# Order of the mixer stage in a two-layer hybrid decoder step: second maxima, first sample's sum, local value loads and gmlp squares moved

## The chip, the cores and the metric

The kernel runs on one core of a Trainium2 chip. The metric is the device time of one execution in microseconds (us). Engines are named TensorE (PE), VectorE (DVE), ScalarE (ACT), GpSimd (POOL) and SyncE (SP), as in the rows; PEld is TensorE's weight load and SPq is SyncE's queue, which issues transfers. All is float32; the large products are split into a high and a low part.

## The reference, cut to what matters

One step of a decoder trunk with two layers. A prompt of 256 tokens and 8 samples with one new token each go through it together. Every layer is FFN, mixer, FFN. The mixer has one input projection and four head groups of 256 channels: A dilated window attention, B attention with forget gates (FoX), C a gated delta rule, D a gated MLP over positions (gmlp). A sample attends to 1024 cached positions.

```python
h = rms_norm(x, g[2]);  parts = project(h, w_in)
# A, sample: keys at distances 0, d, 2d.. < window for (128,1), (512,4), (2048,16), merged by their denominators
o_a = combine_by_denominator([dilated_sample(qa, ka_all, va_all, wb, w, d) for (w, d) in DILATED_PATTERNS])
# B, sample: 8 pages of 128 cached rows, found by page_table, and the own row
o_b = fox_attend(qb, kb_all, vb_all, cum_t, cum_t[:, :, past:], pos)
# C: short convolution, L2 norms, chunked delta rule with a triangular inverse; returns the new state
o_c, s_c, conv_c = gdn_branch(qc, kc, vc, ac, bc, gdn_conv, gdn_s, conv_w, a_log, dt_b)
# D: u = gelu(ud); v = rms_norm(gelu(vd), gv); u * (W_s v + b)
o_d, v_d = gmlp_branch(ud, vd, ws, bs, gv)
y = merge_groups(o_a, o_b, o_c, zc, o_d, out_g, w_out)      # norm per head, gate, output product
```

Outputs are the new activations, and keys, values, gates and states of the prompt and the samples.

## The kernel before

Five engines run one program each, written out by hand in `build`; nothing schedules them but the order of the code and waits on counting semaphores. `S(name)` is a semaphore and `V(name, n)` its value n in this layer. `ch(...)` waits until the instruction in it is done.

FFN stages: weights come in pieces of 1 MB on SyncE's queue, ScalarE makes their high part (L610), VectorE the low part (L1026), and TensorE does three products (L1586 to L1588).

The mixer stage follows the input projection. Its prompt part is on TensorE and VectorE: scores of B and of A in banks 0 to 3 of PSUM, `row_max(0)` and `row_max(1)` on VectorE (L1275 to L1283), `softmax` on ScalarE, transposes of the probabilities on TensorE (L1830) with copies back (`probs_out`, L1289), `delta_front` (L1378 to L1386), `attend_scale` (L1297), and then six levels of the triangular inverse (`LEVELS`). In each level TensorE does y products (L1946), VectorE masks them (L1467), TensorE does z products (L1957, L1958), VectorE subtracts (L1475, L1476). The tables `masked` and `between` name what VectorE does behind the masks and behind the subtractions of each level; `after_y` and `after_z` do so for TensorE.

The sample part is threaded through it. Keys and values of a sample are 11 tiles of 128 rows: 8 pages of the FoX cache, and 3 window tiles of the local cache (`window`, L452 to L454). There are two buffers for keys (`kslot`) and two for values (`vslot`), by sample parity. The work on samples:
- SyncE: `read_pages(b)` reads 8 page numbers into registers (L433); `keys(b)` waits until `s_red` says that the sums of sample b-2 are done, then sends the queries (L474), 8 pages (L462) and 3 window tiles; `vals(b)` waits until `pv_mm` says that TensorE is done with the buffer, then sends 8 pages (L470) and 3 window tiles.
- GpSimd multiplies keys and queries (L1001 to L1004), sample by sample.
- VectorE sums over each head: `sample_add(b)` (L1325, L1327). Then, for pairs j of samples, `sample_bias(j)`, `sample_top(j)`, `sample_shift(j)`.
- ScalarE: `sample_exp(j)` (L785).
- TensorE: `sample_values(j)` (L1898, L1900), after the exponentials and after `v_in0` and `v_in1` say that all 11 value tiles of both samples have landed. It is in `after_z` of levels 1, 3 and 5 for j = 0, 1, 2, and behind the levels for j = 3.
- VectorE: `sample_out(j)` (L1365 to L1367).

For the samples' own key and value VectorE does ten small instructions (L1307 to L1316), between `row_max(0)` and `row_max(1)`. They write `v_own` and `sx`. The gmlp branch needs the sum of squares of v: `gmlp_square` (L1411 to L1415) on VectorE, root on ScalarE (L808, L809), then `gmlp_norm` (L1421 to L1429) on VectorE, its last four instructions for the samples. ScalarE does the squares of the head outputs (L821 to L833) between `sample_exp(1)` and `sample_exp(2)`. The convolution of the samples is scaled by VectorE (L1405) and stored by SyncE (L521), and comes back in other layouts with the states (L525 to L530). SyncE stores keys and values of the prompt (L514 to L517) ahead of `keys(2)`.

Of the kernel before, what the change touches and what calls it, by code (L numbers as in the profile page):

```python
# [23 lines left out]
P = 128  # L24
# [4 lines left out]
B = 8  # L29
# [35 lines left out]
def constants():  # L65
# [71 lines left out]
    "lf_turned": 1, "logf_in": 16, "logf_pre": 1024, "max_diag": 4, "max_turned": 4, "mix_d": 2, "mix_r": 7, "mix_ready": 8, "mix_ss": 6, "mixed": 3, "mm_done0": 77,  # L137
# [13 lines left out]
def build(nc, io):  # L151
# [14 lines left out]
    with ctx:  # L166
# [181 lines left out]
        with nc.Block() as blk:  # L348
            @blk.sync
            def _(sp):  # L350
# [9 lines left out]
                for l in range(DEPTH):  # L360
# [152 lines left out]
                    sp.wait_ge(S("rope"), V("rope", 2))  # L513
                    sp.dma_start(pr(o["fox_k_prompt"][0, l]), tok[:, :, KB_:KB_ + GW]).then_inc(st, 16)  # L514
                    sp.dma_start(pr(o["fox_v_prompt"][0, l]), tok[:, :, VB_:VB_ + GW]).then_inc(st, 16)
                    sp.dma_start(pr(o["swa_v_prompt"][0, l]), tok[:, :, VA:VA + GW]).then_inc(st, 16)
                    sp.dma_start(pr(o["swa_k_prompt"][0, l]), tok[:, :, KA:KA + GW]).then_inc(st, 16)  # L517
# [23 lines left out]
                    vals(5)  # L541
                    sp.dma_start(sm(o["fox_k_sample"][:, l]), smp[:, KB_:KB_ + GW]).then_inc(st, 16)
# [53 lines left out]
            def _(act):  # L596
                ch = Chain(act, "act_ch")
                for l in range(DEPTH):
# [219 lines left out]
                    act.wait_ge(S("mix_d"), V("mix_d", 2))  # L818
# [16 lines left out]
                    sample_exp(2)  # L835
                    sample_exp(3)

                    act.wait_ge(S("mix_ss"), V("mix_ss", 4))
# [4 lines left out]
                    act.wait_ge(S("mix_ss"), V("mix_ss", 5))  # L843
                    ch(act.activation(small[0:B, 104:108], small[0:B, 104:108], ACT.Ln, bias=C("eps", B), scale=1.0 / HD))
                    act.activation(small[0:B, 104:108], small[0:B, 104:108], ACT.Exp, scale=-0.5).then_inc(S("mix_r"), 1)
                    act.wait_ge(S("mix_ss"), V("mix_ss", 6))
# [41 lines left out]
            def _(pool):  # L888
# [5 lines left out]
                for l in range(DEPTH):  # L894
# [72 lines left out]

                    def skp_of(k):
# [23 lines left out]
                    for b in range(B):  # L992
# [3 lines left out]
                        if b == 4:  # L996
                            skp_of(0)
# [18 lines left out]
            def _(dve):  # L1016
                ch = Chain(dve, "dve_ch")
                for l in range(DEPTH):
# [285 lines left out]
                    dve.wait_ge(S("rope"), V("rope", 2))  # L1304
                    own = v_own[:, 0, 0:GW]
                    for k, (qc, kc) in enumerate(((QB_, KB_), (QA, KA))):
                        ch(tt2(own, smp[:, qc:qc + GW], smp[:, kc:kc + GW], ALU.mult))  # L1307
                        ch(red(small[0:B, 112 + 4 * k:116 + 4 * k], own.rearrange("p (h d) -> p h d", h=H), AX.X, ALU.add))
                    ch(ts(small[0:B, 112:120], small[0:B, 112:120], HD ** -0.5, None, ALU.mult))

                    ch(dve.tensor_copy(sx[:, :, :, :], C("own_bias").rearrange("p (b k h) -> p b k h", b=B, k=2)))
                    ch(tt2(sx[0:B, :, :, :].rearrange("p b k h -> p b (k h)"), sx[0:B, :, :, :].rearrange("p b k h -> p b (k h)"),
                           small[0:B, 112:120].unsqueeze(1).broadcast_to([B, B, 8]), ALU.add))
                    dve.memset(v_own[:, :, GW:GW + 1], 1.0)
                    ch(dve.tensor_copy(v_own[:, 0, 0:GW], smp[:, VB_:VB_ + GW]))
                    dve.tensor_copy(v_own[:, 1, 0:GW], smp[:, VA:VA + GW]).then_inc(S("v_own"), 1)  # L1316
# [77 lines left out]
                    probs_out(1)  # L1394
                    attend_scale(1, 0)
                    sample_add(0)
# [10 lines left out]
                    def gmlp_square():  # L1407

                        dve.wait_ge(S("gelu"), V("gelu", 2))
                        for t in range(NT):  # L1410
                            ch(tt2(kb2[:, 0:GW], tok[:, t, VD:VD + GW], tok[:, t, VD:VD + GW], ALU.mult))  # L1411
# [659 lines left out]
```

## Time and profile before

| what | us |
|---|---|
| median of 3 runs | 1471.14 |
| lowest, highest | 1467.81, 1475.22 |
| the profiled execution | 1459.36 |
| its span in the profile | 1457.5 |
| first mixer stage, in the profile | about 308 to 496 |
| second mixer stage | about 1022 to 1206 |

By engine, busy share of the span: TensorE 88%, VectorE 62%, ScalarE 43%, GpSimd 17%. The profiler's page also has the granted clock of TensorE, mean 0.93 of full speed; it is lower in the mixer stages, where TensorE often stands idle. A timeline row gives the start, the busy time, the engine, the line of the kernel, what is written and read, and in brackets the idle time before it with what ended it. A row that merges several instructions (x8) gives their busy time in sum. In a row of waits the three numbers are us in total, times, and the longest.

### The profile page before, as it was taken

The page shows a single profiled execution, that of the slowest core. Times are in us where ns is not written, and L with a number is a line of the kernel's source. Part 1 is how long each engine was busy: PE and PEld are TensorE (multiplying, and loading weights), DVE is VectorE, ACT ScalarE, POOL GpSimd, SP SyncE. Part 2 cuts the span into 40 slices and gives each one's busy share as a digit, 9 for nine tenths or more (in the row PEclk, how much of TensorE's full clock was granted, in tenths as well). Part 3 has the DMA queues.
Part 4 walks back from the last instruction along what each step waited for, and adds up shares of the span by engine and source line. Part 5 has one row for each costly group of instructions (what it writes and reads, how often), then busy time and mean ns, then how long its engine had stood idle before and what let it go on. Part 6 is the DMA issues. An engine that isn't in the chain of part 4 may idle for free.

```text
span 1457.5 us, 27836 instructions
## 1 busy us (share of the span) xinstructions
PE 1282.8 (88%) x9956; PEld 1196.2 (82%) x9956; DVE 903.6 (62%) x1512; ACT 619.8 (43%) x1151; POOL 242.0 (17%) x250
## 2 busy tenths in 40 slices
PE   6999999995755899999999999999676579999998
PEld 5999998984633499999989999999565338899996
DVE  3776447868844557664477663586877454776644
ACT  4655355453020265443465553543612004644443
POOL 2000011025456030000110000110635531100000
PEclk9999999998877699999999999999978767999998
DMA  7555565534456435554655555655435643455563
GB/s 233 163 184 174 147 173 172 174 110 105 143 178 191 141 103 186 178 187 139 187 176 178 173 173 160 188 159 172 115 110 175 186 151 125 138 173 184 154 172 96
DMA packets 286121, 234.17 MB, mean 161 GB/s; under 512 B 19898, under 2 KB 282018, under 8 KB 286056
## 3 DMA queue, kind: packets, MB, share of 16 engines
q1 hardware_dynamic: 286056, 233.37, 52.7%
q8 instruction: 33, 0.54, 0.2%
q14 instruction: 32, 0.26, 0.1%
HBM read 228.65 MB, written 5.37 MB: 161 GB/s over the span
## 4 chain that ended last, share of the span: by engine, by line
PE 71%; DVE 15%; SPq 5%; issue 4%; ACT 3%; DMA 2%; DVEq 0%; ACTq 0%
PE ps L1586 20%; PE ps L1587 20%; PE ps L1588 19%; DVE wlo L1026 2%; PE ps L1898 2%; SPq L470 2%; SPq L462 1%; DVE nlo L1080 1%; DVE s L1325 1%; DVE ps L1063 1%; ACT whi L610 1%; PE ps L1957 1%; DMA vslot<-in_state_swa_v_dram 1%; DMA raw<-in_w_in_dram 1%; PE ps L1923 1%
## 5 line engine op out<-in xcount | busy, mean ns | idle before, releaser
L1586 PE MATMUL ps<-nhi,whi 128*128 128x264 f32 x1936 | 559.5, 289 | 19.3 <-DVE wlo L1026 11.4
L1587 PE MATMUL ps<-nlo,whi 128*128 128x264 f32 x1936 | 552.1, 285 | 0.0
L1588 PE MATMUL ps<-nhi,wlo 128*128 128x264 f32 x1936 | 551.5, 285 | 0.0
L1026 DVE TENSOR_TENSOR wlo<-raw,whi 128x1024 fp32r<-128x1024 f32 (+2 forms) x364 | 380.7, 1087 | 268.3 <-ACT whi L610 267.8
L610 ACT ACTIVATE whi<-raw 128x1024 fp32r<-128x1024 f32 (+2 forms) x364 | 324.9, 942 | 165.7 <-PE ps L1588 104.7
L1586 PEld LDWEIGHTS ps<-nhi,whi 128*128 128x128 f32 x1936 | 368.1, 190 | 28.9 <-DVE nlo L1080 14.4
L1587 PEld LDWEIGHTS ps<-nlo,whi 128*128 128x128 f32 x1936 | 368.5, 190 | 0.2
L1588 PEld LDWEIGHTS ps<-nhi,wlo 128*128 128x128 f32 x1936 | 366.6, 189 | 0.0
L1586 PE MATMUL ps<-hhi,whi 128*128 128x264 f32 x704 | 203.1, 288 | 9.1 <-DVE hlo L1048 9.1
L1588 PE MATMUL ps<-hhi,wlo 128*128 128x264 f32 x704 | 202.2, 287 | 0.0
L1587 PE MATMUL ps<-hlo,whi 128*128 128x264 f32 x704 | 201.8, 287 | 0.0
L1586 PEld LDWEIGHTS ps<-hhi,whi 128*128 128x128 f32 x704 | 134.6, 191 | 10.0 <-issue 9.8
L1588 PEld LDWEIGHTS ps<-hhi,wlo 128*128 128x128 f32 x704 | 134.9, 192 | 0.0
L1587 PEld LDWEIGHTS ps<-hlo,whi 128*128 128x128 f32 x704 | 134.7, 191 | 0.0
L901 POOL TENSOR_TENSOR ss_acc<-sq 128x264 f32<-128x264 f32 x12 | 9.1, 757 | 726.7 <-ACT sq L640 674.6
L630 ACT ACTIVATE hhi<-h_t 128x264 f32 (+1 forms) x88 | 37.4, 425 | 164.2 <-DVE h_t L1045 164.2
L1001 POOL TENSOR_TENSOR kslot<-kslot,q_bc 128x512 f32<-128x512 f32 x64 | 82.1, 1313 | 113.1 <-DMA kslot<-in_state_swa_k_dram 113.1
L905 POOL TENSOR_TENSOR ss_acc<-ss_acc,sq 128x264 f32<-128x264 f32 x66 | 56.7, 860 | 187.7 <-ACT sq L640 166.0
L1898 PE MATMUL ps<-vslot,s 128*4 128x257 f32 x352 | 41.2, 487 | 44.9 <-DMA vslot<-in_state_swa_v_dram 44.9
L1048 DVE TENSOR_TENSOR hlo<-h_t,hhi 128x264 f32 (+1 forms) x88 | 38.2, 434 | 59.9 <-ACT hhi L630 59.9
L1898 PEld LDWEIGHTS ps<-vslot,s 128*4 128x4 f32 x352 | 12.9, 98 | 68.4 <-issue 60.6
L785 ACT ACTIVATE s<-s 128x104 f32<-128x104 f32 x8 | 2.3, 290 | 156.8 <-DVE s L1358 156.8
(345 smaller groups left out, 1465.6 us busy)
## 6 DMA issues: line engine op xcount, KB each, us to landing
raw<-in_ffn_gate_dram SPq DMA_DIRECT2D x44, 1024.0 KB, 5.3
raw<-in_ffn_up_dram SPq DMA_DIRECT2D x44, 1024.0 KB, 5.4
raw<-in_ffn_down_dram SPq DMA_DIRECT2D x64, 704.0 KB, 4.5
raw<-in_w_in_dram SPq DMA_DIRECT2D x24, 1024.0 KB, 5.7
kslot<-in_cache_fox_k_dram SPq DMA_DIRECT2D x128, 128.0 KB, 2.8
vslot<-in_cache_fox_v_dram SPq DMA_DIRECT2D x128, 128.0 KB, 2.8
raw<-in_w_out_dram SPq DMA_DIRECT2D x8, 1024.0 KB, 5.1
kslot<-in_state_swa_k_dram SPq DMA_DIRECT2D x32, 128.0 KB, 2.8
```

Source lines behind the costliest of these rows:

```text
L462: sp.dma_start(kslot[:, i, g, :], io["cache_fox_k"][bass.ds(page_of[b, g], 1), l].rearrange("o p h d -> p (o h d)")).then_inc(S(f"k_in{i}" ...
L470: sp.dma_start(vslot[:, i, g, 0:GW], io["cache_fox_v"][bass.ds(page_of[b, g], 1), l].rearrange("o p h d -> p (o h d)")).then_inc(S(f"v_in{ ...
L610: act.activation(whi[s][:, a:b], raw[s][:, a:b], ACT.Copy).then_inc(S(f"w_hi{s}"), 1)
L630: act.activation(hhi[:, bass.ds(2 * j + f, 1), :].rearrange("p o n -> p (o n)"), h_t[:, f, :], ACT.Copy).then_inc(S("h_hi"), 1)
L905: ins = tt_(ss_acc[:, :], ss_acc[:, :], sq8[:, t, :], ALU.add)
L1001: ins = tt_(kslot[:, i, g:g + 2, :], kslot[:, i, g:g + 2, :], q_bc[:, i, GW:512].unsqueeze(1).broadcast_to([P, 2, GW]), ALU.mult)
L1026: tt2(wlo[s][:, a:b], raw[s][:, a:b], whi[s][:, a:b].bitcast(F32), ALU.subtract).then_inc(S(f"w_lo{s}"), 1)
L1048: tt2(hlo[:, at, :].rearrange("p o n -> p (o n)"), h_t[:, f, :], hhi[:, at, :].rearrange("p o n -> p (o n)").bitcast(F32), ALU.subtract).t ...
L1586: mm(out, wh, hi_, start=first, stop=False)
L1587: mm(out, wh, lo_, start=False, stop=False)
L1588: return mm(out, wl, hi_, start=False, stop=last)
L1898: mm(out, s13[:, u, FOX_PG * m + g, :], vslot[:, i, NPG * m + g, :], start=(g == 0), stop=False)
```

## The change

Nothing is computed in another way, but for the samples' squares of the gmlp branch, which are summed in two halves. In every layer:
- VectorE does `row_max(1)` directly behind `row_max(0)` and the bias copies. The ten instructions for `v_own` stand behind `probs_out(1)` instead, ahead of `attend_scale(1, 0)`.
- `sample_add(0)` stands ahead of `probs_out(0)` instead of behind `attend_scale(1, 0)`. In the tables, `sample_add(2)` and `(3)` move to level 1, `(4)` to level 2, `(5)` to level 3 and `(6)` to level 4.
- The window tiles of the values for samples 2 to 7 are issued by ScalarE, behind `sample_exp(0)`, `(1)` and `(2)`, each time after a wait for `pv_mm`. SyncE issues them for samples 0 and 1 alone.
- SyncE does `read_pages(6)` and `keys(3)` ahead of the convolution's store, `keys(4)` behind it, `keys(5)` ahead of `vals(2)` and `keys(6)` behind `vals(3)` and ahead of `read_pages(7)`. The prompt's keys and values are stored behind `vals(5)`.
- ScalarE does the gmlp squares with an accumulating output, right behind the root for the convolution, and scales the samples' v. GpSimd does the rest of the samples' gmlp ahead of its product for sample 3 (`b == 3`). The state product `skp_of(0)` moves from `b == 4` to `b == 6`.

```diff
@@ SyncE @@
-                        window(vslot, i, b, "state_swa_v", S(f"v_in{i}"))
+                        if not use:
+                            window(vslot, i, b, "state_swa_v", S(f"v_in{i}"))
...
-                    sp.wait_ge(S("rope"), V("rope", 2))
-                    sp.dma_start(pr(o["fox_k_prompt"][0, l]), tok[:, :, KB_:KB_ + GW]).then_inc(st, 16)
...
                     read_pages(5)
                     keys(2)
+                    read_pages(6)
+                    keys(3)
                     sp.wait_ge(S("s_conv"), V("s_conv", 1))
                     sp.dma_start(d_cn.rearrange("c b (h e) -> (c b h) e", h=H), cv[:, 8, :]).then_inc(S("regroup"), 16)
-                    keys(3)
+                    keys(4)
...
-                    read_pages(6)
-                    keys(4)
+                    keys(5)
                     vals(2)
-                    keys(5)
                     vals(3)
+                    keys(6)
                     read_pages(7)
-                    keys(6)
                     keys(7)
                     vals(4)
                     vals(5)
+                    sp.wait_ge(S("rope"), V("rope", 2))
+                    sp.dma_start(pr(o["fox_k_prompt"][0, l]), tok[:, :, KB_:KB_ + GW]).then_inc(st, 16)
...
@@ ScalarE @@
-                    act.wait_ge(S("mix_ss"), V("mix_ss", 3))
-                    ch(act.activation(small[:, 24:27], small[:, 24:27], ACT.Ln, bias=C("eps"), scale=1.0 / GW))
-                    act.activation(small[:, 24:27], small[:, 24:27], ACT.Exp, scale=-0.5).then_inc(S("mix_r"), 1)
+                    for t in range(NT):
+                        act.activation(kb_n[:, t, :], tok[:, t, VD:VD + GW], ACT.Square, accum_out=small[:, 24 + t:25 + t])
...
+                    act.activation(smp[:, VD:VD + GW], smp[:, VD:VD + GW], ACT.Copy, scale=small[0:B, 26:27]).then_inc(S("mix_r"), 1)
+
+                    def value_windows(j):
+
+                        act.wait_ge(S("pv_mm"), V("pv_mm", j))
+                        for i in range(2):
+                            a = io["state_swa_v"][2 * j + i, l].rearrange("r h d -> r (h d)")
+                            sem = S(f"v_in{i}")
+                            act.dma_start(vslot[:, i, NPG, 0:GW], a[PAST - P:PAST, :]).then_inc(sem, 16)
...
                     sample_exp(0)
+                    value_windows(1)
                     act.wait_ge(S("state_in"), V("state_in", 16 * (B + 4 + 2 + 4)))
                     act.activation(small[:, 120:121], gb[:, 0:1], ACT.Exp).then_inc(S("sg"), 1)
                     sample_exp(1)
+                    value_windows(2)
...
                     sample_exp(2)
+                    value_windows(3)
                     sample_exp(3)
@@ GpSimd @@
-                        if b == 4:
+                        if b == 3:
+                            sample_gmlp()
+                        if b == 6:
                             skp_of(0)
@@ VectorE @@
+                    sample_add(0)
                     probs_out(0)
                     delta_front()
                     probs_out(1)
+                    dve.wait_ge(S("rope"), V("rope", 2))
+                    own = v_own[:, 0, 0:GW]
...
                     attend_scale(1, 0)
-                    sample_add(0)
...
-                    masked = {0: [lambda: add(1), lambda: sample_bias(0)], 1: [lambda: sample_shift(0)], 2: [lambda: out(0), lambda: add(3), lambda: sample_bias(1)],
-                              3: [lambda: sample_shift(1), lambda: add(4)], 4: [lambda: out(1), lambda: add(5), lambda: sample_bias(2)],
-                              5: [lambda: sample_shift(2), lambda: add(6)]}
-                    between = {0: [lambda: sample_top(0), conv_scale, gmlp_square], 1: [gmlp_norm, lambda: add(2)], 2: [lambda: sample_top(1), gmlp_mix],
-                               3: [lambda: state_sum(0)], 4: [lambda: sample_top(2), state_value], 5: [state_new]}
+                    masked = {0: [lambda: add(1), lambda: sample_bias(0)], 1: [lambda: sample_shift(0), lambda: add(2)], 2: [lambda: out(0), lambda: sample_bias(1)],
+                              3: [lambda: sample_shift(1), lambda: add(5)], 4: [lambda: out(1), lambda: sample_bias(2)], 5: [lambda: sample_shift(2)]}
+                    between = {0: [lambda: sample_top(0), conv_scale], 1: [lambda: add(3), gmlp_norm], 2: [lambda: sample_top(1), lambda: add(4), gmlp_mix],
+                               3: [lambda: state_sum(0)], 4: [lambda: sample_top(2), lambda: add(6), state_value], 5: [state_new]}
```

The built programs show the order on the engines. First VectorE at the head of the mixer, before; `s_115` is the tile `s13` of the samples' sums, `proj` holds the second scores, `ptr` the probabilities:

```order
L1303 COPY bias<-const 128x8x12
L1307 TENSOR_TENSOR v_own<-smp 8x256
...
L1316 COPY v_own<-smp 8x256
L1281 SCALAR_TENSOR_TENSOR proj<-ps,const 128x1536
L1282 TENSOR_REDUCE small<-proj 128x4
L1283 TENSOR_REDUCE small<-proj 128x4
L1391 COPY proj<-ps 128x4x128
L1289 COPY ptr<-ps 128x512 x3
L1378 TENSOR_TENSOR tt<-ps,ys 128x2x2x64 x2
```

and the same place with the change:

```order
L1338 COPY bias<-const 128x8x12
L1316 SCALAR_TENSOR_TENSOR proj<-ps,const 128x1536
L1317 TENSOR_REDUCE small<-proj 128x4
L1318 TENSOR_REDUCE small<-proj 128x4
L1413 COPY proj<-ps 128x4x128
L1347 TENSOR_REDUCE s_115<-kslot 128x32
L1349 TENSOR_REDUCE s_115<-kslot 128x12
L1324 COPY ptr<-ps 128x512 x3
L1400 TENSOR_TENSOR tt<-ps,ys 128x2x2x64 x2
...
L1324 COPY ptr<-ps 128x512
L1421 TENSOR_TENSOR v_own<-smp 8x256
```

The maxima (three rows on `proj`) follow the bias copy, the two sums of `sample_add(0)` stand ahead of the three probability copies, and `v_own` comes behind the fourth.

ScalarE behind the root for the convolution, before:

```order
L805 ACTIVATE small<-small 64x1
L808 ACTIVATE small<-small,const 128x3
L809 ACTIVATE small<-small 128x3
L785 ACTIVATE s_115<-s_115 128x104
L813 ACTIVATE small<-gb 128x1
L785 ACTIVATE s_115<-s_115 128x104
L821 ACTIVATE ptr,small<-otok 128x64 x24
```

and with the change:

```order
L817 ACTIVATE smp<-smp,small 8x256
L786 ACTIVATE s_115<-s_115 128x104
L825 DMA vslot<-in_state_swa_v_dram 128x256
L826 DMA vslot<-in_state_swa_v_dram 128x256
L827 DMA vslot<-in_state_swa_v_dram 64x256
...
L832 ACTIVATE small<-gb 128x1
L786 ACTIVATE s_115<-s_115 128x104
...
L842 ACTIVATE ptr,small<-otok 128x64 x24
```

Six transfers now stand behind each of the first three exponentials (those on `s_115`), ahead of the exponential of the gate and of the squares of the heads.

## Rows read from the trace of the kernel before

**Rows 1.** Who waited for whom, 320 to 500 us, first mixer stage.

```profile
POOL kslot L1001 <- DMA kslot<-in_state_swa_k_dram: 58.2, 6, 24.0
...
PE ps L1898 <- DMA vslot<-in_state_swa_v_dram: 23.6, 2, 13.0
```

**Rows 2.** The waits of SyncE's queue, 330 to 500 us.

```profile
SPq L474 <- DVE s L1327: 21.5, 3, 14.6
...
SPq L470 <- PE ps L1900: 5.4, 1, 5.4
```

**Rows 3.** Timeline of VectorE, first mixer stage.

```profile
334.14 0.98 DVE L1307 TENSOR_TENSOR v_own<-smp 8x256 f32<-8x256 f32 x1
...
342.65 1.74 DVE L1281 SCALAR_TENSOR_TENSOR proj<-ps,const 128x1536 f32<-128x1536 f32 x1
...
345.02 1.21 DVE L1283 TENSOR_REDUCE small<-proj 128x4 f32<-128x1024 f32 x1
...
360.18 0.69 DVE L1297 TENSOR_TENSOR otok<-ps,small 128x512 f32<-128x512 f32 x1 [2.96 <-PE ps L1845]
...
367.83 0.93 DVE L1327 TENSOR_REDUCE s<-kslot 128x12 f32<-128x768 f32 x1
...
373.47 0.30 DVE L1405 TENSOR_SCALAR cv<-cv,small,const 96x64 f32<-96x64 f32 x1
...
377.28 1.27 DVE L1467 TENSOR_TENSOR ys<-ps,const 128x512 f32<-128x512 f32 x2
```

**Rows 4.** Timeline of GpSimd, end of the product for sample 1.

```profile
346.95 1.26 POOL L1004 TENSOR_TENSOR kslot<-kslot,q_bc 128x512 f32<-128x512 f32 x1
```

**Rows 5.** Timeline of SyncE's queue, first mixer stage: issues, not landings.

```profile
339.12 2.50 SPq L512 DMA_DIRECT2D gb<-d_gate  x4
...
363.95 0.34 SPq L474 DMA_DIRECT2D q_bc<-d_q  x1
...
369.46 0.51 SPq L454 DMA_DIRECT2D kslot<-in_state_swa_k_dram  x1
...
380.60 1.06 SPq L525 DMA_DIRECT2D kq<-d_cn  x2
...
384.15 3.81 SPq L530 DMA_DIRECT2D state<-in_state_gdn_s_dram  x8
...
417.55 0.47 SPq L454 DMA_DIRECT2D vslot<-in_state_swa_v_dram  x1
422.84 0.33 SPq L474 DMA_DIRECT2D q_bc<-d_q  x1
...
429.95 0.50 SPq L454 DMA_DIRECT2D kslot<-in_state_swa_k_dram  x1
...
447.39 3.85 SPq L470 DMA_DIRECT2D vslot<-in_cache_fox_v_dram  x8
...
452.23 0.47 SPq L454 DMA_DIRECT2D vslot<-in_state_swa_v_dram  x1
```

**Rows 6.** Timeline of TensorE: `sample_values(1)` and the start of `sample_values(2)`.

```profile
420.67 3.60 PE L1898 MATMUL ps<-vslot,s 128*4 128x257 f32 x28 [13.01 <-DMA vslot<-in_state_swa_v_dram]
...
428.67 0.70 PE L1900 MATMUL ps<-v_own,s 8*4 8x257 f32 x4
...
455.69 3.59 PE L1898 MATMUL ps<-vslot,s 128*4 128x257 f32 x28 [10.55 <-DMA vslot<-in_state_swa_v_dram]
```

**Rows 7.** Second layer: timelines of SyncE's queue and of TensorE.

```profile
1052.83 2.90 SPq L512 DMA_DIRECT2D gb<-d_gate  x4
...
1166.02 3.59 PE L1898 MATMUL ps<-vslot,s 128*4 128x257 f32 x28 [8.91 <-DMA vslot<-in_state_swa_v_dram]
```

**Rows 8.** Timeline of ScalarE: the squares of the heads and `sample_exp(2)`.

```profile
404.83 0.24 ACT L821 ACTIVATE ptr<-otok 128x64 f32<-128x64 f32 x1
...
412.49 0.41 ACT L833 ACTIVATE small<-small 128x16 f32<-128x16 f32 x3
...
443.83 0.29 ACT L785 ACTIVATE s<-s 128x104 f32<-128x104 f32 x1 [30.93 <-DVE s L1358]
```

More of the change, by code:

```diff
@@ L541, in _ @@
                     vals(5)
+                    sp.wait_ge(S("rope"), V("rope", 2))
+                    sp.dma_start(pr(o["fox_k_prompt"][0, l]), tok[:, :, KB_:KB_ + GW]).then_inc(st, 16)
+                    sp.dma_start(pr(o["fox_v_prompt"][0, l]), tok[:, :, VB_:VB_ + GW]).then_inc(st, 16)
+                    sp.dma_start(pr(o["swa_v_prompt"][0, l]), tok[:, :, VA:VA + GW]).then_inc(st, 16)
+                    sp.dma_start(pr(o["swa_k_prompt"][0, l]), tok[:, :, KA:KA + GW]).then_inc(st, 16)
                     sp.dma_start(sm(o["fox_k_sample"][:, l]), smp[:, KB_:KB_ + GW]).then_inc(st, 16)
@@ new lines, in _ @@
+                    ch(act.activation(st_s[0:B, :, :].rearrange("b a v -> b (a v)"), smp[:, VD:VD + 128], ACT.Square, accum_out=small[0:B, 26:27]))
+                    ch(act.activation(st_s[0:B, :, :].rearrange("b a v -> b (a v)"), smp[:, VD + 128:VD + GW], ACT.Square, accum_out=small[0:B, 27:28]))
+                    ch(act.activation(small[0:B, 26:27], small[0:B, 26:27], ACT.Identity, bias=small[0:B, 27:28]))
+                    act.activation(small[:, 24:26], small[:, 24:26], ACT.Ln, bias=C("eps"), scale=1.0 / GW)
@@ L966, in masks, with sample_gmlp @@
                             C("strict").unsqueeze(1).broadcast_to([P, 8, P]), ALU.mult).then_inc(S("dts"), 1)
+                    def sample_gmlp():
+                        pool.wait_ge(S("mix_r"), V("mix_r", 3))
+                        tt_(smp[:, VD:VD + GW], smp[:, VD:VD + GW], gv[0:B, :], ALU.mult).then_inc(S("gmlp_v"), 1)
+                        pool.wait_ge(S("gmlp_v"), V("gmlp_v", 1))
+                        od = smp_o[:, 768:1024].rearrange("p (h d) -> p h d", h=H)
+                        eight = lambda ap: ap.unsqueeze(2).broadcast_to([B, H, HD])
+                        ch(tt_(od, smp[:, VD:VD + GW].rearrange("p (h d) -> p h d", h=H), eight(ws0[:, 0, :]), ALU.mult))
+                        ch(tt_(od, od, eight(ws0[:, 1, :]), ALU.add))
+                        tt_(smp_o[:, 768:1024], smp_o[:, 768:1024], smp[:, UD:UD + GW], ALU.mult).then_inc(S("mix_s"), 1)
                     def skp_of(k):
@@ L1303, in _ @@
                     dve.tensor_copy(bias[:, :, NPG:NKT, :], C("window").rearrange("p (g h) -> p g h", h=H).unsqueeze(1).broadcast_to([P, B, CACHE_T, H]))
[L1304 to L1316, printed above, removed]
                     row_max(1)
@@ L1394, in _ @@
                     probs_out(1)
+                    dve.wait_ge(S("rope"), V("rope", 2))
+                    own = v_own[:, 0, 0:GW]
+                    for k, (qc, kc) in enumerate(((QB_, KB_), (QA, KA))):
+                        ch(tt2(own, smp[:, qc:qc + GW], smp[:, kc:kc + GW], ALU.mult))
+                        ch(red(small[0:B, 112 + 4 * k:116 + 4 * k], own.rearrange("p (h d) -> p h d", h=H), AX.X, ALU.add))
+                    ch(ts(small[0:B, 112:120], small[0:B, 112:120], HD ** -0.5, None, ALU.mult))
+                    ch(dve.tensor_copy(sx[:, :, :, :], C("own_bias").rearrange("p (b k h) -> p b k h", b=B, k=2)))
+                    ch(tt2(sx[0:B, :, :, :].rearrange("p b k h -> p b (k h)"), sx[0:B, :, :, :].rearrange("p b k h -> p b (k h)"),
+                           small[0:B, 112:120].unsqueeze(1).broadcast_to([B, B, 8]), ALU.add))
+                    dve.memset(v_own[:, :, GW:GW + 1], 1.0)
+                    ch(dve.tensor_copy(v_own[:, 0, 0:GW], smp[:, VB_:VB_ + GW]))
+                    dve.tensor_copy(v_own[:, 1, 0:GW], smp[:, VA:VA + GW]).then_inc(S("v_own"), 1)
                     attend_scale(1, 0)
-                    sample_add(0)
                     dve.wait_ge(S("s_silu"), V("s_silu", 1))
@@ L1405, in conv_scale @@
                         ts(cv[:, 8, :], cv[:, 8, :], small[0:96, 0:1], C("q_scale", 96), ALU.mult, ALU.mult).then_inc(S("s_conv"), 1)
[L1407 to L1411, printed above, removed]
-                            ch(red(small[:, 24 + t:25 + t], kb2[:, 0:GW], AX.X, ALU.add))
-                        ch(dve.memset(small[:, 26:27], 1.0))
-                        ch(tt2(kb2[0:B, 0:GW], smp[:, VD:VD + GW], smp[:, VD:VD + GW], ALU.mult))
-                        red(small[0:B, 26:27], kb2[0:B, 0:GW], AX.X, ALU.add).then_inc(S("mix_ss"), 1)
                     def gmlp_norm():
@@ L1422, in gmlp_norm @@
                         ins.then_inc(S("v_n"), 1)
-                        stt(smp[:, VD:VD + GW], smp[:, VD:VD + GW], small[0:B, 26:27], gv[0:B, :], ALU.mult, ALU.mult).then_inc(S("gmlp_v"), 1)
-                        dve.wait_ge(S("gmlp_v"), V("gmlp_v", 1))
-                        od = smp_o[:, 768:1024].rearrange("p (h d) -> p h d", h=H)
-                        eight = lambda ap: ap.unsqueeze(2).broadcast_to([B, H, HD])
-                        ch(tt2(od, smp[:, VD:VD + GW].rearrange("p (h d) -> p h d", h=H), eight(ws0[:, 0, :]), ALU.mult))
-                        ch(tt2(od, od, eight(ws0[:, 1, :]), ALU.add))
-                        tt2(smp_o[:, 768:1024], smp_o[:, 768:1024], smp[:, UD:UD + GW], ALU.mult).then_inc(S("mix_d"), 1)
                     def gmlp_mix():
@@ L1927, in turned_state @@
                     def turned_state():
-                        pe.wait_ge(S("mix_d"), V("mix_d", 2))
+                        pe.wait_ge(S("mix_d"), V("mix_d", 1))
                         state_mm(0)
```

19 lines of the change are left out of this document (11 added, 8 removed).

## The prediction, made before the run

> **What bounds the kernel now.** I read the views from the outside in. The page's engine rows say TensorE is busy for 88% of the span, but that is a mean over unlike stages: the FFN stages are solid TensorE, and the two mixer stages are not. So I went to the waits of the first layer's mixer, from 320 to 500 us. There the reader is to see two waits for data: GpSimd stands 58.2 us for the sliding-window keys, TensorE 23.6 us for the sliding-window values [rows 1]. Who is late there, the transfers or their issue? The waits of SyncE's queue answer: it stood 21.5 us itself for VectorE's sums over the keys (`sample_add`), the longest time 14.6 us [rows 2]. A key buffer is free only when `sample_add` of two samples earlier is done. VectorE does `sample_add(0)` late, behind work that nothing there needs yet. The mixer is therefore a latency chain: VectorE's order, then key transfers, then products, then sums, then value transfers, then `sample_values`. It ends twice in a transfer: `sample_values(1)` starts at 420.67 and `sample_values(2)` at 455.69, both when a window transfer lands [rows 6].
>
> **The head of the stage, part by part.** VectorE's ten small instructions for the sample's own key and value take from 334.14 to 342.65, 8.5 us, and the second maxima (3.5 us, to 346.15) stand behind them, though their scores are ready [rows 3]. The change puts the maxima first: their end moves from 346.15 to 337.65. Between the maxima and the three probability copies it puts `sample_add(0)`, 3.1 us (before, from the end of L1297 at 360.87 to the free of the buffer at 363.95) [rows 3, 5]. In that gap VectorE waited for TensorE's transposes anyway for some 1.2 us, so the copies end 6.5 us earlier than before rather than 8.5, and the wait for TensorE's next product (1.1 us before) vanishes too: the delta part runs 7.6 us earlier. The ten moved instructions now stand ahead of `attend_scale(1)`, where VectorE idled 2.96 us [rows 3]. What do they cost there? At most 8.5 us as now, at least what fits the idle time, nothing. I take 3.4 us, an estimate from small instructions beside no product, 0.2 to 0.4 us each as L1405's 0.30 [rows 3]: GpSimd's second product ends at 348.2 [rows 4] and the block starts at about 349.5. That leaves 0.5 us uncovered. With `sample_add(0)` gone from behind it, the sum over the head is 7.6 - 0.5 + 3.1 = 10.2 us: `sample_add(1)` ends at 358.5 instead of 368.76 [rows 3].
>
> **The port of the two engines.** One instruction of the head moves into GpSimd's products: L1383, two operands in SBUF, at about 344. The first of the ten, with both operands in SBUF too, took 0.98 us beside GpSimd's work [rows 3]. For L1383 the bounds are nothing and one instruction of GpSimd, 1.26 us [rows 4]; since only this one stands there I count nothing and keep 1.2 us for the range. The Trainium skill (SBUF — State Buffer, Who interferes with whom) says that a VectorE instruction with two SBUF inputs and a GpSimd instruction that reads SBUF exclude each other for a whole instruction. The trace fits it, and by that rule the sum would be 2.4 us smaller over both layers.
>
> **SyncE's queue becomes the bound.** With that head, I lay out SyncE's issues from the end of the gate transfers at 341.62 [rows 5] in their new order. The terms, per layer:
> - page numbers of samples 5, 6, 7: before, the queue stood from 418.02 to 422.84 for one sample's eight, 4.8 us, with its sums long done [rows 5]; 3 x 4.8 = 14.4.
> - six key sets: one is 6.0 us (363.95 to 369.97), the slowest 7.6 (422.84 to 430.45) [rows 5]; the twelve of both layers average 6.3, and I take that: 37.8.
> - four value sets without their window: 3.85 us and a small gap each [rows 5], 15.6. The three window issues of a set, 1.4 us (from 451.24 to 452.70), go to ScalarE.
> - the convolution's store, and the group of keys, values and states (380.60 to 387.96) [rows 5]: 7.8.
> Sum 75.6 us. On top come its waits. Set 3 is ready to issue at 341.62 + 4.8 + 6.3 + 4.8 = 357.5 and waits for `sample_add(1)`: 1.0. Set 4 is ready at 365.2 and waits for `sample_add(2)`, which follows `sample_add(1)` by the 5.0 us to the end of L1405 [rows 3], two masks, the shift and its own 3.1, so at 368.1: 2.9. I round to 4.0. Later sets find their sums done by 4 us or more. Value set 5 is thus issued at 341.62 + 79.6 = 421.2 and lands 3.0 us later, as before (452.70 to 455.69) [rows 5, 6]: `sample_values(2)` starts at 424.2 instead of 455.7, **31.5 us** earlier. In the second layer the queue starts at 1055.73 and the same instruction at 1166.02 [rows 7]; 1055.73 + 82.6 = 1138.3, so **27.7 us**. What follows `sample_values(2)` is unchanged and depends on little else.
>
> **What is moved at no cost, and its cover.** The four prompt outputs (four issues of about 0.5 us) now stand ahead of the last value sets; SyncE waited 5.4 us for TensorE there [rows 2], and pays 2 us if that wait is gone. The squares that VectorE loses (L1411 to L1415, between 373.77 and 377.28) [rows 3] are 3.5 us off VectorE, and the sample's share of the norm goes too, but once SyncE's queue sets the pace, they lie in slack: I count nothing for them. GpSimd takes over four small instructions before its product for sample 3, where it waits for keys; ScalarE does the squares ahead of `sample_exp(0)`, for which it waits anyway. If either cover were gone, the price would be about the 3.5 us that VectorE paid.
>
> **Sum.** 31.5 + 27.7 = 59.2 us off the profiled execution's 1459.4: 1400.2. That execution is 0.8% below the median of the three runs, 1471.1; from the median the same saving gives **1412 us**, which I forecast. A measurement of this kernel can tell about 0.5%, some 7 us, from no change.
>
> **Rivals.**
> - *The transfers, not their issue, set the pace.* With fewer gaps, and ScalarE's windows beside SyncE's sets, every set could take what the slowest took [rows 5]: six times 1.3 and, by the same ratio, four times 0.8, 11 us a layer. The gain is 37.2: 1434. For it: one set did take 7.6; against it: most sets run at the issue's own pace. The Trainium skill (DMA: Bandwidth & Descriptors, Issuing engines are not separate DMA queues) says that all issuing engines share the same 16 DMA engines, and that a second one saves issue time alone. By it the moved windows would be worth their 5.6 us a layer only where the issue bounds. No row of before shows two queues at work.
> - *More than the sum.* The 4 us of waits go, sets take 6.0: 5.8 us a layer more, 1459.4 - 70.8 = 1389 from the faster base.
> - *Only the head is won*, 2 x 10.2, since another wait, say GpSimd for the third product, absorbs the rest: 1451. Against it: the long wait for keys is released by the head itself.
> - *Slower.* ScalarE now waits for TensorE's values and issues six transfers before it may do the head squares and `sample_exp(2)`. The squares take 8.1 us (404.83 to 412.90) [rows 8]. `sample_values(1)`, after value set 3 lands at 399.7, ends by 408.4 even at its 8.7 us of before (420.67 to 429.37) [rows 6]. `sample_exp(2)` is wanted at 424.2, so 15.8 us are there: each issue may cost (15.8 - 8.1)/6 = 1.3 us for nothing. `sample_shift(2)` lets it start no sooner than some 14.3 us after the values anyway (429.4 to 443.83) [rows 8]. SyncE pays 0.47 to 0.51 for such an issue [rows 5], so this is close only if ScalarE is three times as slow. From (7.7 + 29.6)/6 = 6.2 us an issue the gain is gone; at 7 us the kernel is 2 x 4.7 slower: 1481.
>
> **Numbers.** Forecast 0.56 (its own range 1400 to 1424), slower transfers 0.20, more than the sum 0.14, head alone 0.05, ScalarE's queue 0.05, of which 0.03 beyond 0.5% and 0.02 within it. So faster 0.95, same 0.02, slower 0.03. The range is 1388, the stronger case from the faster base, to 1436, slower transfers and the port's 2.4 us; it leaves out the last two cases and a little of each end.
>
> **What would show it.** VectorE's L1281 starts at about 334.1 instead of 342.65. SyncE's first key set starts at about 346.4 instead of 363.95, and the queue runs with gaps of under 3 us to value set 5. `sample_values(2)` starts near 424 and 1138, less in both layers by about 30. GpSimd's long wait of 24.0 us [rows 1] shrinks to some 7. ScalarE's window issues show about 0.45 us each, and none of its waits is followed by a late `sample_exp`. I am wrong if key sets last over 7 us, if TensorE waits for ScalarE before L1898, or if the queue still stands long for sums.

## The result, and the profile after

| us | before | after |
|---|---|---|
| median of all runs | 1469.47 (1462.03 to 1475.22) | **1410.78** (1408.83 to 1412.02) |
| the profiled execution | 1459.36 | 1412.02 |

The ratio is 0.9602, 95% interval 0.9556 to 0.9648: faster, by 58.7 us between the medians. The forecast was 1412 us. But the two profiled executions, against which the sum was made, differ by only 47.3 us, where the sum said 59.2. Both numbers have to be explained.

Busy time by stage, of the kernel before (first mixer, FFN stages between, second mixer, FFN at the end; then the granted clock, DMA share and GB/s):

```profile
308.00:496.00 188.00, 122.47 (x877) 91.51 (x875) 125.51 (x248) 45.46 (x155) 85.28 (x75) 0.79 0.49 142
496.00:1022.00 526.00, 513.56 (x4096) 502.58 (x4095) 324.52 (x504) 260.73 (x412) 35.64 (x46) 0.99 0.55 168
1022.00:1206.00 184.00, 120.37 (x875) 92.12 (x872) 125.96 (x248) 44.66 (x155) 85.03 (x75) 0.80 0.49 145
```

and with the change:

```profile
308.00:469.00 161.00, 120.97 (x881) 91.39 (x880) 111.79 (x237) 48.12 (x167) 86.51 (x81) 0.81 0.60 168
469.00:995.00 526.00, 513.85 (x4095) 502.63 (x4094) 324.49 (x504) 261.15 (x412) 35.71 (x46) 0.99 0.55 168
995.00:1159.00 164.00, 119.56 (x873) 91.57 (x870) 118.09 (x237) 47.88 (x167) 85.35 (x79) 0.83 0.55 162
```

The windows are cut where the products over the heads begin (495.54 and 1205.69 before, 468.67 and 1159.07 after) and 16 us ahead of the second mixer's first queries. The FFN stages are the same 526 us with the same busy times. The first mixer is 27 us shorter, the second 20: only there is something to explain. TensorE's busy share rose from 88 to 91%, with the same work.

Waits, 320 to 500 us, with the change, against [rows 1]:

```profile
POOL kslot L1036 <- DMA kslot<-in_state_swa_k_dram: 35.0, 6, 8.7
PE ps L1915 <- DMA vslot<-in_cache_fox_v_dram: 5.6, 2, 4.4
```

The longest wait for keys fell from 24.0 to 8.7 us, the wait for values from 23.6 to 5.6. SyncE's own waits for the sums, 320 to 500 us, against the 21.5 us of [rows 2]:

```profile
SPq L475 <- DVE s L1349: 5.5, 2, 4.0
```

Timeline of SyncE's queue, first mixer, against [rows 5]:

```profile
333.00 6.79 SPq L470 DMA_DIRECT2D vslot<-in_cache_fox_v_dram  x8
...
341.34 2.51 SPq L513 DMA_DIRECT2D gb<-d_gate  x4
348.77 0.33 SPq L475 DMA_DIRECT2D q_bc<-d_q  x1
...
360.74 0.34 SPq L475 DMA_DIRECT2D q_bc<-d_q  x1
...
372.19 0.34 SPq L475 DMA_DIRECT2D q_bc<-d_q  x1
...
417.71 7.73 SPq L470 DMA_DIRECT2D vslot<-in_cache_fox_v_dram  x16
```

From the gates' end at 343.85 to value set 5 at 425.44 it is 81.6 us; the prediction laid out 79.6. VectorE's head, against [rows 3]:

```profile
334.71 1.74 DVE L1316 SCALAR_TENSOR_TENSOR proj<-ps,const 128x1536 f32<-128x1536 f32 x1
...
344.44 1.38 DVE L1405 TENSOR_TENSOR tt<-const,tt 128x512 f32<-128x512 f32 x1
...
351.52 0.40 DVE L1421 TENSOR_TENSOR v_own<-smp 8x256 f32<-8x256 f32 x1
...
359.77 0.94 DVE L1349 TENSOR_REDUCE s<-kslot 128x12 f32<-128x768 f32 x1
```

The ten moved instructions take 3.04 us (to 354.56) where they took 8.5: they now stand where GpSimd is idle. `sample_add(1)` ends at 360.71, 8.05 us earlier than before. TensorE, the third pair of samples in both layers, against [rows 6, 7]:

```profile
428.71 3.59 PE L1915 MATMUL ps<-vslot,s 128*4 128x257 f32 x28 [1.23 <-DMA vslot<-in_cache_fox_v_dram]
...
1119.22 3.38 PE L1915 MATMUL ps<-vslot,s 128*4 128x257 f32 x28 [1.27 <-DMA vslot<-in_cache_fox_v_dram]
```

So `sample_values(2)` starts 27.0 us earlier in the first layer (forecast 31.5), and 46.8 in the second, of which 19.8 are its own (forecast 27.7). The second layer's head shows one reason. VectorE, then GpSimd's product for sample 1 beside it:

```profile
1030.78 4.51 DVE L1405 TENSOR_TENSOR tt<-const,tt 128x512 f32<-128x512 f32 x1
```

```profile
1027.86 4.97 POOL L1036 TENSOR_TENSOR kslot<-kslot,q_bc 128x512 f32<-128x512 f32 x4
1032.76 0.76 POOL L1038 TENSOR_TENSOR kslot<-kslot,q_bc 128x256 f32<-128x256 f32 x1
1033.44 1.30 POOL L1039 TENSOR_TENSOR kslot<-kslot,q_bc 128x512 f32<-128x512 f32 x1
```

L1405 (L1383 before the change, where it stands behind GpSimd's product and takes 0.69 us) lasts 4.51 us. It ends at 1035.29, 0.55 us after the end of that product (1034.74): it stood through the rest of one GpSimd instruction and three more. TensorE then waited for VectorE's L1408, which stands behind L1405, and did its next products at the lower of its two levels (1.2 GHz), 0.63 us for what takes 0.39 us at 2.4 GHz in the first layer. TensorE in the second layer, and then the same products in the first:

```profile
1036.63 1.69 PE L1882 MATMUL ps<-const,tt 128*128 128x128 f32 x8 [2.29 <-DVE qkt L1408]
1039.67 0.63 PE L1861 MATMUL ps<-tok,ptr 128*128 128x64 f32 x2
```

```profile
352.23 0.39 PE L1861 MATMUL ps<-tok,ptr 128*128 128x64 f32 x2
```

### The profile page after: what moved, and what is told of

Read it like the earlier page. It is cut to its first block, busy times and chain, and to the rows that moved or that the text cites. A ratio compares the mean times of both kernels' runs of the same rounds, so it can differ in the third digit from the quotient of the medians.

```text
span 1410.2 us, 27848 instructions
## 1 busy us (share of the span) xinstructions
PE 1280.8 (91%) x9956; PEld 1196.1 (85%) x9956; DVE 882.0 (63%) x1490; ACT 625.6 (44%) x1175; POOL 243.1 (17%) x258
## 4 chain that ended last, share of the span: by engine, by line
PE 72%; DVE 12%; SPq 7%; issue 4%; DMA 2%; ACT 2%; DVEq 0%; POOL 0%; ACTq 0%; POOLq 0%
PE ps L1603 21%; PE ps L1604 21%; PE ps L1605 21%; SPq L470 2%; SPq L462 2%; DVE wlo L1061 2%; PE ps L1915 1%; DVE nlo L1115 1%; DVE s L1347 1%; DVE ps L1098 1%; PE ps L1963 1%; DMA raw<-in_w_in_dram 1%; ACT whi L611 1%; PE ps L1940 1%; PE ps L2022 1%
## 5 line engine op out<-in xcount | busy, mean ns | idle before, releaser
L626 ACT ACTIVATE s_t<-s_t 128x264 f32<-128x264 f32 x88 | 35.9, 426 | 57.7 <-DVE s_t L1073 57.6
L637 ACT ACTIVATE yt<-ps 128x264 f32 (+1 forms) x48 | 18.8, 392 | 81.4 <-PE ps L1605 81.2
L1073 DVE TENSOR_TENSOR s_t<-ps,ptr 128x264 f32<-128x264 f32 x88 | 36.2, 428 | 29.7 <-ACT ptr L674 21.0
```

Source lines behind the costliest of these rows:

```text
L626: act.activation(s_t[:, f, :], s_t[:, f, :], ACT.Silu).then_inc(S("silu"), 1)
L1073: tt2(s_t[:, f, :], ps[:, f, 0:N], r_pre, ALU.mult).then_inc(S("gate_taken"), 1)
```

## The experiments

Each kernel ran on one chip together with the kernel before. There are three such groups: runs 2, 3, 5 and 6; runs 1, 4, 7 and 9; runs 8, 10, 11 and 12. Differences below are between medians, of one group where nothing else is said.

**1. The kernel before once more.**

> The kernel before once more, for a second profiled execution of it and the span and clock of every run. The medians of before and after differ by 56 to 59 us, the first profiled executions by 47. Theory: the 1459.4 of the first profiled execution was a short one, and this one, at about 1468, is longer in the waits of the two mixer stages (key sets late, sets of transfers that take longer), not in the FFN stages. Rival: it is longer in the FFN stages or at a lower clock there, which would have nothing to do with the change.

Measured: median 1465.73 (1463.47 to 1472.34), profiled execution 1464.63. By stage:

```profile
308.00:497.00 189.00, 126.85 (x879) 95.36 (x879) 126.94 (x248) 45.68 (x155) 85.58 (x78) 0.77 0.50 142
497.00:1023.00 526.00, 513.81 (x4093) 502.77 (x4094) 324.48 (x505) 260.53 (x412) 35.69 (x46) 0.99 0.55 168
1023.00:1211.00 188.00, 121.34 (x875) 90.99 (x873) 126.23 (x248) 44.80 (x155) 85.08 (x75) 0.80 0.49 141
```

All of the 5.3 us lies in the mixers, 0.9 in the first and 4.4 in the second (from the first queries to the products over the heads). The twelve executions show what goes with a long one: in six the mean granted clock was 0.930 to 0.933, and they took 1463.5 to 1466.1 us; in six it was 0.924 to 0.928, and they took 1465.3 to 1472.3. Which of the two causes the other is not shown. The theory holds for place; its figure of 1468 was not met in this execution.

**2. The changed kernel once more.**

> The changed kernel once more, as the base for its variants on the same chip. Both theories: 1411 us. What is asked of it: whether the two profiled executions' difference of 47.3 us or the medians' 58.7 us comes again; if the smaller one does, the kernel before ran slow in some of its executions and the sum of the prediction was 12 us too large.

Measured: 1411.81 (1409.85 to 1416.68), before 1468.21, so 56.4 us. Its profiled execution took 1416.68, the longest of its five. Between the second pair of profiled executions (runs 1 and 2, of two groups) lie 48.0 us, where the first pair had 47.3; between medians 56.4, where it was 58.7. Both come again. The first profile of before, 1459.36, is shorter than any other execution of it, the second is just under its median, and both profiles of after are the longest of their groups. In this one the granted clock of the second mixer (995 to 1163 us) was 0.77, against 0.83 in the first profile of after, and TensorE did the products of the third pair at the lower of its two levels, 1.2 instead of 2.4 GHz:

```profile
1122.71 3.60 PE L1915 MATMUL ps<-vslot,s 128*4 128x257 f32 x16
```

where that first profile has 1.91 us for the same 16 products (at 1123.06). Both pairs of profiles thus show a saving that is 8 to 11 us smaller than the medians'.

**3. VectorE's head as before, in the changed kernel.**

```diff
-                    sample_add(0)
                     probs_out(0)
                     delta_front()
                     probs_out(1)
-                    dve.wait_ge(S("rope"), V("rope", 2))
...
                     attend_scale(1, 0)
+                    sample_add(0)
```

(and the ten instructions ahead of `row_max(1)` again.)

> The changed kernel with the order of VectorE's head as before (the ten small instructions ahead of the second maxima, the sums of sample 0 behind attend_scale). Theory: key set 2 is issued at about 363.5 instead of 348.8; SyncE's waits of 1.2 and 4.0 us vanish, so value set 5 comes some 10.5 us later, 21 us in both layers: 1432. Rival (the new order of the queue won it all, and the head lies in slack): 1411 to 1416.

Measured: 1432.88 (1430.45 to 1439.06), 21.1 us slower than run 2. Key set 2 is issued at 364.18, where the theory put it (363.5), and value set 5 ends at 435.42 instead of 425.44:

```profile
364.18 0.34 SPq L475 DMA_DIRECT2D q_bc<-d_q  x1
```

**4. VectorE's head of the change, in the kernel before.** The same two moves, made in the kernel before.

> The kernel before with VectorE's head as in the change, and nothing else. Theory (the change is head and order of the queue together): the head's 8 to 10 us a layer reach the end of the stage, 16 to 20 us faster than before, 1448 to 1452; with the 21 us that the head is worth in the changed kernel, head and the rest add up. Rival (the long wait for keys just moves, to the wait for the sums of sample 2 ahead of key set 4): under 5 us.

Measured: 1450.59 (1445.84 to 1459.77) against 1467.98, ratio 0.989 (0.9869 to 0.9911), 17.4 us faster. The head is worth 17 to 21 us; the rest of the change is worth 35.3 us (run 3 against before, 1468.21). Of these 35.3 us, run 5 puts 10.8 on the windows; no run separates the new order of the sets from the moved sums. The profiled execution of this kernel, 1459.77, is the longest of its seven and 9 us above their median, so nothing is read from it.

**5. All windows by SyncE.**

```diff
-                        if not use:
-                            window(vslot, i, b, "state_swa_v", S(f"v_in{i}"))
+                        window(vslot, i, b, "state_swa_v", S(f"v_in{i}"))
...
-                    value_windows(1)
```

> The changed kernel with all window tiles of the values issued by SyncE again. Theory (the issues of SyncE's queue set the pace up to value set 5): four sets become 1.4 us longer each, 5.6 us a layer, so about 11 us slower than the changed kernel, 1422. Rival (transfers, or GpSimd's products, set the pace): within 3 us of it, 1411 to 1414.

Measured: 1422.65 (1421.65 to 1424.68), 10.8 us slower. The issues of value set 5 end at 431.0 instead of 425.4, and TensorE waits for just its window tile again, 6.3 us:

```profile
433.73 3.29 PE L1901 MATMUL ps<-vslot,s 128*4 128x257 f32 x28 [6.32 <-DMA vslot<-in_state_swa_v_dram]
```

So here the issues set the pace. The largest rival (0.20) had staked on the transfers, with every set as slow as the slowest, 7.6 us for a key set; in the first profile of after the twelve key sets take 6.0 to 7.0 us. The Trainium skill (DMA: Bandwidth & Descriptors, Issuing engines are not separate DMA queues) grants a second issuing engine the issue time alone; here that time was 5.6 us a layer, 11.2 in both, and the 10.8 us agree with it.

**6. The gmlp squares on VectorE.** ScalarE's, GpSimd's and VectorE's parts are as before the change, with `gmlp_square` behind `conv_scale`.

> The changed kernel with the gmlp squares and the samples' gmlp on VectorE again. As the prediction counted it: nothing, 1411, since SyncE's queue sets the pace. Rival, from the trace of the changed kernel, where SyncE waits 4.0 us for the sums of sample 2 ahead of key set 4: the 3.5 us of squares stand between those sums and what precedes them, and show in full, 3.5 us a layer, 1418.

Measured: 1413.96 (1413.26 to 1415.14), 2.2 us slower by the medians, but inside the range of run 2 (1409.85 to 1416.68): neither side is shown. Key set 4 starts at 373.59 instead of 372.19 in the first layer, but key set 3 before it is 2.0 us late already (362.76 instead of 360.74): VectorE's second maxima start at 336.79 instead of 334.71, behind a wait of 1.90 us for TensorE, long before the squares. From key set 3 to key set 4 it is 10.8 and 11.9 us in the two layers here, and 8.5 to 11.6 in the four layers of both profiles of the changed kernel. So the traces don't separate it either. What is refuted is a cost of 3.5 us in each layer, 7 in all.

**7. Prompt outputs early.**

> The changed kernel with the four prompt outputs back ahead of key set 2. Theory: they stand on the path from the first key set to the sums of sample 2, 2.1 us a layer, 4 us slower, 1415. Rival: SyncE's waits of 1.2 and 4.0 us behind them absorb it, 1411.

Measured: 1412.39 (1404.72 to 1417.60), ratio to before 0.9627, where run 2 had 0.9618. With that spread neither side is shown.

**8. The subtraction L1405 later.**

> The changed kernel with L1405 (the subtraction with both operands in SBUF, 0.69 us alone, up to 4.5 us beside GpSimd's product for sample 1) moved behind the two products of t = 0, 1.3 us later. Theory (it waits for instructions of GpSimd's product and is late whenever that product still runs): where it stood 3.8 us before it now stands about 1.3 us less, its end stays, and the kernel's time within 2 us of 1411. Rival (its length is its own, or TensorE's): it stays at up to 4.5 us and ends 1.3 us later.

Measured: 1411.42 (1409.28 to 1413.61). It took 1.38 and 1.37 us in the two layers. VectorE, and GpSimd's last instruction of the product beside it:

```profile
1032.95 1.37 DVE L1409 TENSOR_TENSOR tt<-const,tt 128x512 f32<-128x512 f32 x1
```

```profile
1032.49 1.28 POOL L1039 TENSOR_TENSOR kslot<-kslot,q_bc 128x512 f32<-128x512 f32 x1
```

It ends 0.55 us after that product in both layers, as it did in the unmoved place in the second layer. So its length is GpSimd's doing, not its own: where GpSimd's product is over (before, and run 3) it takes 0.69 us in every layer. But its end isn't always that of the product. In the first layer of after it took 1.38 us and ended at 345.82, while the product ran to 348.86; and in the first layer of run 2 it took 0.69 us in the middle of the product, and GpSimd's L1038 beside it took 1.21 us instead of 0.72. The moved instruction started when GpSimd was in its last instruction (1032.49), so it could not show a long stand. The kernel's time did not change: ratio 0.962, against 0.9618 in run 2.

**9. The delta part's transfers by ScalarE.** SyncE's block of 14 issues (keys, values and states) goes behind `sample_exp(0)`:

```diff
                     sample_exp(0)
+                    act.wait_ge(S("regroup"), V("regroup", 64))
+                    for k in range(2):
+                        act.dma_start(kq16[:, k, :], d_cn[k].rearrange("b (g e) -> (b g) e", e=16)).then_inc(S("state_in"), 16)
...
                     value_windows(1)
```

> The changed kernel with the 14 transfers of keys, values and states of the delta part issued by ScalarE, behind the first exponential, instead of SyncE. Theory (SyncE's issues set the pace): 7.8 us of issues leave the queue; the sums of sample 3 at 377.9 are done by the time that key set 5 could go (378.8), so 6 to 8 us a layer, 12 to 16 us faster than the changed kernel, 1396 to 1399. Rival (transfers or GpSimd's products take over as the bound): 0 to 4 us.

Measured: **1394.81** (1393.53 to 1399.48) against 1467.98, ratio 0.951 (0.9486 to 0.9534); the changed kernel stood at 0.9618 (0.9587 to 0.9648) in run 2. This is 16 to 17 us faster than the change, twice the 8.0 us of issues; from the first and the second profile of after to this one's 1399.48 it is 12.5 and 17.2 us. ScalarE does in 7.5 us what SyncE did in 8.0:

```profile
369.78 0.88 ACTq L823 DMA_DIRECT2D kq<-d_cn  x2
370.70 2.47 ACTq L825 DMA_DIRECT2D v<-d_cn  x4
373.20 4.14 ACTq L828 DMA_DIRECT2D state<-in_state_gdn_s_dram  x8
```

**10. The gates too.**

> The kernel with the delta part's 14 transfers on ScalarE, and the four transfers of the gates (gb, 2.5 us ahead of key set 2) there too. Theory: page numbers of sample 5 and key set 2 come 2.5 us earlier, and with them the sums of sample 2: 2.5 us a layer, 1390. Rival (behind the first gain another wait is the bound: in the first layer TensorE no longer waited for a value set before the third pair): 0 to 2 us, 1393 to 1395.

Measured: 1402.20 (1397.07 to 1409.66): 5 us **slower** than run 9 by the ratios to before (0.9547 against 0.951, whose intervals overlap) and 8 us slower than run 11 of its group. Neither theory had it. The profiled execution is the longest of the five (1409.66), but its first layer shows what happened. Key set 2 did start earlier, at 343.65 instead of 347.17. So GpSimd's product for sample 2 began at 352.58 instead of 355.66, and met the ten instructions on VectorE. Timeline of VectorE in this kernel:

```profile
354.01 1.22 DVE L1425 COPY sx<-const 128x64 f32<-128x64 f32 x1
355.27 1.21 DVE L1426 TENSOR_TENSOR sx<-sx,small 8x64 f32<-8x64 f32 x1
356.52 1.25 DVE L1429 COPY v_own<-smp 8x256 f32<-8x256 f32 x1
```

and in the kernel of run 9, before GpSimd starts:

```profile
353.33 0.20 DVE L1425 COPY sx<-const 128x64 f32<-128x64 f32 x1
353.56 0.21 DVE L1426 TENSOR_TENSOR sx<-sx,small 8x64 f32<-8x64 f32 x1
353.81 0.28 DVE L1429 COPY v_own<-smp 8x256 f32<-8x256 f32 x1
```

The block takes 7.0 us instead of 3.0 in both layers, `sample_add(1)` ends at 365.3 instead of 360.3, and key set 3 goes out 5.0 us later; the third pair's values start at 426.10 instead of 421.52. The gain at the head turned into a collision behind it. In the second layer the block is as long, but L1405 took 4.50 us in run 9 and 1.61 here, which hides part of the loss: `sample_add(1)` ends 28.9 us after the start of the second maxima here, 30.8 in run 9. So only the first layer shows the collision cleanly. No run moves the block by itself, so how much of the 5 to 8 us it makes is not shown.

**11. Value sets 2 and 3 by ScalarE.**

> The kernel with the delta part's 14 transfers on ScalarE, and value sets 2 and 3 there as well, with the page numbers read by ScalarE. Theory of the queue as the only bound: 7.7 us of issues a layer less for SyncE, up to 1380. Rival (key set 6 then waits for the sums of sample 4, which were ready only 1.6 us before it; the bound is the chain of products and sums): 1 to 2 us a layer, 1391 to 1394.

Measured: 1394.25 (1392.07 to 1402.23), ratio 0.9507 (0.9473 to 0.9541). Against run 9 (another group, ratio 0.951) no difference: the 7.7 us of issues that left SyncE's queue bought nothing measurable. They became waits for the sums. SyncE's waits, 320 to 500 us, in run 9 and then here:

```profile
SPq L475 <- DVE s L1349: 6.1, 3, 2.8
```

```profile
SPq L475 <- DVE s L1355: 13.1, 3, 6.5
```

So without the delta part's transfers the queue is no longer the bound. The chain of GpSimd's products and VectorE's sums is the theory left, argued and not shown by a run. TensorE's longest wait for another engine's data inside the levels is for VectorE's masks, behind the sums of sample 5, which wait for GpSimd:

```profile
PE ps L1980 <- DVE ys L1490: 7.9, 1, 7.9
```

The changed kernel has that wait already, 7.6 us, so it doesn't tell the two kernels apart.

**12. All three.**

> Gates, delta part and value sets 2 and 3 on ScalarE together. Queue theory: 1375. Rival (chain of products and sums): 1386 to 1391, with the gates' 2.5 us a layer the only part that shortens that chain at its head.

Measured: 1399.72 (1389.97 to 1404.31), where neither theory had it, and 5.5 us above run 11, with ranges that overlap. The block collides here too (7.2 and 4.9 us). Moving the ten instructions once more, behind `sample_add(1)`, into GpSimd's pause, was not tried.

## Why the prediction was right, and where it was off

The mechanism held. The maxima start at 334.71 (334.1 forecast). Key set 2 no longer waits for sums. SyncE's queue is the bound up to value set 5 (runs 5 and 9: issues added cost their full time, issues removed gave it back), and ScalarE's windows cost 0.34 to 0.61 us each, so that the rival of ScalarE's queue was far off. The rival "only the head" is refuted by runs 3 and 4 (the head is 17 to 21 us of 56 to 59), "slower transfers" by run 5 and the key sets' 6.0 to 7.0 us; "more than the sum" did not occur, since SyncE still waited for sums.

Two of the named signs missed. The queue was to run with gaps of under 3 us, and its longest waits for sums were 4.0 and 5.0 us. `sample_values(2)` of the second layer was to start near 1138, which leaves out the first layer's gain; with it the forecast means 1107, and it started at 1119.22.

The sizes:

- **The head.** The ten instructions took 3.04 us, against the estimate of 3.4. `sample_add(1)` came 8.05 us earlier, not 10.2; 0.56 us of the gap is the stage's own later start, and nearly all of the rest is a wait of 1.99 us for TensorE ahead of the first `attend_scale`, where VectorE had waited 0.42: the head counted nothing for that.
- **The queue's start.** It was taken from the trace of before, 341.62, and was 343.85, since the pages of value set 1 took 6.79 us to issue instead of 5.13. That is not the change's doing: in the second profile of the kernel before they took 6.53, in the profiles of all runs 5.1 to 7.2. What sets it is open.
- **"For L1383 the bounds are nothing and one instruction of GpSimd."** This bound failed. The trace of before shows no stand beyond one instruction (the copy L1315 took 2.32 us beside one instruction of GpSimd of 2.33). But in the 12 layers of six profiled kernels of this order (both profiles of after, runs 5, 6, 7 and 9) it took 0.69 to 4.52 us, so it waited up to 3.8. In the second layer of the first profile it was 4.51, and the wait for `sample_add(1)` ahead of key set 3 was 5.0 us instead of 1.0.
- **TensorE's level, which the head had no term for.** L1405 isn't the whole of that wait. In the second profile of after, it took 0.69 us in the first layer and 4.33 in the second, and SyncE waited 5.2 and 2.1 us for the same sums, the other way round. From the start of the second maxima to the end of `sample_add(1)` the forecast has 24.4 us (334.1 to 358.5). It was 23.8 in the first layer of run 5, with L1405 at 1.35 and TensorE's products ahead of both `attend_scale` at 2.4 GHz; 26.7 in the second layer of run 2, with L1405 at 4.33, behind which VectorE waited no more for TensorE at the first `attend_scale`; 26.0 and 26.6 in the first layers of after and run 2, with L1405 at 1.38 and 0.69, where TensorE did part of these products at 1.2 GHz; and 30.4 in the second layer of after, with both. What sends TensorE to the lower level there stays open.
- **The sets.** In the second layer two value sets took 8.65 us and key set 4 took 7.0, where 7.8 and 6.3 were counted.

Together the queue took 81.6 and 85.4 us where 79.6 were laid out; with its later starts that makes 27.0 + 19.8 = 46.8 us in one pair of profiles instead of 59.2. The medians, which the forecast was stated for, gave 56.4 and 58.7. The forecast carried a sum made against one short execution over to the median. That execution lay 10.1 us below the median of before, and the one of after 1.2 above its own: these are the 11.4 us between 47.3 and 58.7. In the second pair it was 3.6 and 4.9. By the medians the sum is too large by 1 to 3 us, by the profiled pairs by 11 to 12. Why the profiled executions of before lie low in their groups and those of after high is not shown. So the hit to 1.2 us is in part luck: against the pair of executions that it can be laid beside, the sum was a quarter too large.

## What to carry to other kernels

When a queue stands long for a result, look at what stands ahead of that result on its engine, and then lay out the whole queue again with the wait gone: here the wait was worth about 20 us, and the order and the length of the queue behind it 35. While issue time was the bound, the issues that an idle engine took over were worth their full length, until another chain was longer (run 9 gained 16 us, run 11 nothing more). When a prediction is made from one profiled execution, look where that execution lies among the others: two pairs of profiles showed 47 to 48 us where the medians showed 56 to 59. Before moving a transfer earlier, ask which engine it wakes, and what that engine then runs beside.

## What the runs showed of the hardware

A VectorE instruction can wait for several GpSimd instructions in a row, not for one: L1405 took between 0.69 and 4.52 us, the 4.51 us through four instructions of GpSimd. The other way round, GpSimd's L1038 took 1.21 us instead of 0.72 when L1405 got in first (first layer of run 2). The Trainium skill (SBUF — State Buffer, Who interferes with whom) has the exclusion by whole instructions, and that copies can take part in it; the trace agrees (run 10: copies of 0.20 and 0.28 us took 1.22 and 1.25). It also says that VectorE's reductions do not contend, and they did not: L1347 took 2.27 to 2.29 us beside GpSimd and without it. How many instructions it waits through when they follow each other closely changed from execution to execution.

The eight page issues of value set 0 took 3.67 or 3.68 us in every profile, those of value set 1 behind them on the same queue 5.13 to 7.19. Executions of one kernel in one group differed by up to 14 us (run 12: 1389.97 to 1404.31), the longer ones mostly with a lower mean granted clock (0.947 and 0.942 for these two). The stretch between the two mixers took 540.8 to 543.3 us in all profiles.
